# Two branch products in three fp32r passes, modulation chunks one merge sooner, the last norm by halves

## Chip, core and metric

The kernel runs on one core of one Trainium2 chip. The metric is the device time of one execution in microseconds (us), the lower the better. A core has a matrix engine (PE, with its weight loads listed apart as PEld), a vector engine (DVE), a scalar engine (ACT), a general engine (POOL) and SyncE (SP), whose queue issues nearly all DMAs here. The engines run their own instruction streams and meet only at semaphores. PE writes into eight PSUM banks of 128 x 512 fp32.

## What is computed

Two blocks of two layers each, on 256 tokens of width 1024, all in fp32. The change touches the first block and the last line of the second. One layer of the first block, cut to what matters:

```python
mod = c_act @ ada_w[l] + ada_b[l]                 # 3 x 1024 values: shift, scale, gate
h = rms_norm(x, pre_norm[l]) * (1 + scale) + shift
p = split_proj(h @ w_in[l])                       # projections, then "merge": 3 x 1024 columns
ret = rms_norm(retention(...)) * silu(p["ret_g"])     # [256, 512]
dsa = dsa_attention(...) * silu(p["dsa_g"])           # [256, 512]
gl  = rms_norm(gla(...)) * silu(p["gla_g"])           # [256, 512]
g = sigmoid(p["merge"]).reshape(B, S, 3, D)
y = g[:, :, 0] * (ret @ w_br_ret[l]) + g[:, :, 1] * (dsa @ w_br_dsa[l]) + g[:, :, 2] * (gl @ w_br_gla[l])
x = x + gate * rms_norm(y @ w_out[l], post_norm[l])
...
return rms_norm_2(x, final_g)                     # the last line of the second block
```

## The kernel before

**Weights.** All weights stream from HBM in chunks of up to 2 MB into a ring of three slots (`ring`). The table `RING1` names, for each layer of the first block, the 27 chunks in the order of loading, with width and slot. SP issues them in this order, one by one; ahead of each it waits until the chunk that held the slot has been used (`previous1`). A chunk whose slot is busy holds up all that stand behind it in SP's queue.

**Products.** An fp32 product of PE (`project`, and the branch products at L1081) reads a weight chunk as it is. A product in split passes reads three fp32r copies: ACT rounds the weights to a high part (L1605), DVE subtracts to get the rest (L2358), and PE adds high x high, rest x high and high x low in one bank (L1021). The merges from `SPLIT_FROM[l]` on (2 in layer 0, 1 in layer 1) are done so, in two halves of the k dimension; so are the output products. A merge chunk gives one 128 x 512 result for each of two token tiles (t = 0, 1), with banks chosen in `units_of_layer1`.

**Order.** The stage of interest is written out by hand. PE, ACT and DVE each run a loop over g = 0 to 17: g = 0 to 5 are the two tiles of ret_g, dsa_g and gla_g, g = 6 to 17 those of merge0 to merge5. In the gap after each g stand the small products of the three branches: the GLA scores `gla_scores(g)` go to banks 2 and 3, which DVE empties in `gla_take(g)` (L2300, L2305, L2309) before the next scores can start. At g = 11, 12, 13 PE transposes the results of retention, GLA and DSA (`retT`, `glaT`, `dsaT`), which ACT copies to SBUF. After the loop come the three branch products, br0, br1, br2.

**Modulation chunks.** The six chunks ada0 to ada5 of a layer compute `mod`: 0 to 3 shift and scale of the layer ahead, 4 and 5 the gate of this one. All six of layer 0, and 4 and 5 of layer 1, are summed by DVE (`chunk_sum`: L2067, then seven times L2070). Chunks 0 to 3 of layer 1 (`summed_on_pe`) go through PE ("rows", L719, 16 records), then a copy by ACT to SBUF. Either way PE then turns the sum into columns (`ada1`, L727, 8 records) and DVE adds them to `mod`. SP may reload the slot only when the sum is done. In the kernel before, chunk_sum(m) stands on DVE at merge m+1, and that of chunk 5 after the loop; the columns of chunk m follow merge m+1 on PE, and use bank 1, which merges 0 to 3 use too.

**Last norm.** For each token tile DVE adds two halves to X (L2498, L2500), ACT squares and sums the row of 1024 (L1885), DVE scales, ACT takes the root (L1887), DVE inverts and multiplies all 1024 columns (L2760), and SP stores 512 KB.

## Time and profile before

| | |
|---|---|
| median of 3 runs | 1077.6 us (1077.05 to 1078.86) |
| the profiled execution's own time | 1079.21 us |
| its span in the trace | 1077.4 us |
| mean granted clock of PE | 0.994 of full speed |
| PE busy (matmul) | 1042.0 us, 97% of the span |
| DVE, ACT busy | 601.1 us (56%), 477.9 us (44%) |
| branch products, layers 0 and 1 | 263.6 to 305.9 us, 566.6 to 608.9 us of the span |

The profiled execution was 1.6 us longer than the median of the timed runs. Its span leaves out 1.8 us around the program. PE's busy time is modelled from the starts of matmuls and overlaps, so pace is best read from start to start.

### The profile page before, as it was taken

Reading aid. Unit: us, or ns where it says so; the run is one execution under the profiler, and the core shown is the slowest. Engines: PE = TensorE matmul, PEld = TensorE weight load, DVE = VectorE, ACT = ScalarE, POOL = GpSimd, SP = SyncE. Lnnn points to the kernel's source line nnn. Section 1 sums busy time; section 2 is a strip of 40 time slices with the busy share of each in tenths; the row PEclk is TensorE's granted clock in tenths of the full one; section 3 lists DMA queues with packets and bytes.
Section 4 is the critical chain, followed back from the end, with each engine's and each line's share of the span. In section 5 each row is a group of like instructions: output and inputs, shape, how many; then the busy total and the mean of one; then the engine's idle time right before and its main releaser. Section 6 shows DMA issues by size and latency. Waiting matters only on the chain.

```text
span 1077.4 us, 13519 instructions
## 1 busy us (share of the span) xinstructions
PE 1042.0 (97%) x5208; PEld 757.8 (70%) x5208; DVE 601.1 (56%) x1177; ACT 477.9 (44%) x942; POOL 76.6 (7%) x103
## 2 busy tenths in 40 slices
PE   7999999999999999999999999999999999999997
PEld 5688875777467888857874587777677888556553
DVE  2429966595655299754454744236745555245742
ACT  3437547462134365476540353246535423225641
POOL 3001110000000020110000000500000001230000
PEclk9999999999999999999999999999999999999999
DMA  9645432476624355335467362422642015242000
GB/s 385 277 164 203 182 134 101 156 293 276 251 90 170 140 208 203 113 130 219 189 243 304 121 234 79 156 98 79 235 157 103 1 40 220 112 156 98 2 1 39
DMA packets 13743, 171.29 MB, mean 159 GB/s; under 512 B 1504, under 2 KB 1760, under 8 KB 3056
## 3 DMA queue, kind: packets, MB, share of 16 engines
q1 hardware_dynamic: 13216, 168.82, 41.0%
q10 hardware_dynamic: 464, 1.61, 0.4%
q8 instruction: 42, 0.69, 0.2%
q14 instruction: 21, 0.17, 0.0%
HBM read 169.37 MB, written 1.05 MB: 158 GB/s over the span
## 4 chain that ended last, share of the span: by engine, by line
PE 83%; DVE 7%; ACT 6%; DMA 2%; issue 1%; SPq 0%; DVEq 0%; ACTq 0%
PE bank L786 15%; PE bank L1132 8%; PE bank L1081 8%; PE bank L1021 7%; PE bank L1179 6%; PE bank L756 5%; PE bank L1138 5%; PE bank L1114 4%; PE bank L1316 3%; PE bank L764 3%; PE bank L866 3%; PE bank L1393 2%; PE bank L719 2%; PE bank L1381 1%; PE bank L727 1%
## 5 line engine op out<-in xcount | busy, mean ns | idle before, releaser
L1505 ACT ACTIVATE whi<-ring 128x512 fp32r<-128x512 f32 x120 | 73.6, 631 | 65.3 <-PE bank L786 65.3
L2169 DVE TENSOR_TENSOR wlo<-ring,whi 128x512 fp32r<-128x512 f32 x120 | 82.2, 708 | 32.8 <-ACT whi L1505 32.5
L786 PE MATMUL bank<-whi,xhi 128*128 128x512 f32 (+1 forms) x256 | 98.2, 384 | 1.3 <-ACT dsag L1428 1.3
L786 PE MATMUL bank<-wlo,xhi 128*128 128x512 f32 (+1 forms) x256 | 96.4, 377 | 0.0
L786 PE MATMUL bank<-whi,xlo 128*128 128x512 f32 (+1 forms) x256 | 96.4, 376 | 0.0
L764 PE MATMUL bank<-ring,hT 128*128 128x512 f32 (+1 forms) x160 | 61.2, 536 | 0.2 <-ACT hT L1448 0.2
L1138 PE MATMUL bank<-ring,hT 128*128 128x256 f32 (+2 forms) x224 | 57.9, 418 | 3.3 <-ACT hT L1471 2.3
L1021 PE MATMUL bank<-merge_high,xhi 128*128 128x512 f32 x144 | 58.2, 404 | 1.6 <-ACT retqkv L1428 1.1
L1021 PE MATMUL bank<-ring_low,xhi 128*128 128x512 f32 x144 | 56.9, 395 | 0.0
L1021 PE MATMUL bank<-merge_high,xlo 128*128 128x512 f32 x144 | 56.9, 395 | 0.0
L786 PEld LDWEIGHTS bank<-whi,xhi 128*128 128x128 f32 x256 | 48.2, 188 | 11.8 <-ACT dsag L1428 1.6
L786 PEld LDWEIGHTS bank<-whi,xlo 128*128 128x128 f32 x256 | 48.2, 188 | 8.9
L786 PEld LDWEIGHTS bank<-wlo,xhi 128*128 128x128 f32 x256 | 48.2, 188 | 8.2
L1138 PEld LDWEIGHTS bank<-ring,hT 128*128 128x128 f32 x224 | 38.9, 190 | 21.4 <-issue 16.3
L2358 DVE TENSOR_TENSOR ring_low<-ring,merge_high 128x1024 fp32r<-128x1024 f32 x36 | 42.5, 1222 | 18.7 <-ACT merge_high L1605 18.5
L1132 PE MATMUL bank<-ring_low,xhi 128*128 128x512 f32 x128 | 50.5, 394 | 0.0
L764 PEld LDWEIGHTS bank<-ring,hT 128*128 128x128 f32 x160 | 29.7, 190 | 26.4 <-issue 20.5
L1663 ACT ACTIVATE out_high<-ring 128x1024 fp32r<-128x1024 f32 x16 | 15.6, 1044 | 65.6 <-DMA ring<-in_weights 65.6
L2070 DVE SCALAR_TENSOR_TENSOR retqkv<-ring,cst,retqkv 128x512 f32<-128x512 f32 x56 | 42.1, 752 | 2.0
L1605 ACT ACTIVATE merge_high<-ring 128x1024 fp32r<-128x1024 f32 x36 | 36.0, 1052 | 9.6 <-PE bank L1021 9.6
L1132 PE MATMUL bank<-wide,xhi 128*128 128x512 f32 x96 | 39.0, 406 | 0.2 <-DVE ring_low L2520 0.2
L1179 PE MATMUL bank<-whi,xhi 128*128 128x512 f32 x96 | 38.5, 401 | 0.0
(414 smaller groups left out, 2198.3 us busy)
## 6 DMA issues: line engine op xcount, KB each, us to landing
ring<-in_weights SPq DMA_DIRECT2D x73, 2048.0 KB, 8.1
ring<-in_weights SPq DMA_DIRECT2D x5, 1024.0 KB, 5.0
ring<-in_weights SPq DMA_DIRECT2D x2, 1360.0 KB, 10.3
ring<-in_weights SPq DMA_DIRECT2D x1, 1536.0 KB, 8.3
kk<-in_k SPq DMA_DIRECT2D x1, 1120.0 KB, 7.7
X<-in_x SPq DMA_DIRECT2D x1, 1024.0 KB, 14.6
kc<-in_k ACTq DMA_DIRECT2D x1, 1024.0 KB, 10.6
X<-in_context SPq DMA_DIRECT2D x1, 1024.0 KB, 10.1
```

Of the source, the lines that this page charges most:

```text
L756: mm = pe.transpose(ps[0:n, i * P:(i + 1) * P], blk, ident[:])
L764: mm = pe.matmul(ps[:, 0:width], hT[:, k, t * P:(t + 1) * P], ring[:, slot, k * stride + w0:k * stride + w0 + width], start=(k == 0), stop ...
L786: mm = pe.matmul(o[:, 0:width], a, b[:, q % BUFFERS, at], start=(k == 0 and m == 0), stop=(k == KD - 1 and m == 2))
L1021: mm = pe.matmul(o[:, :], a, b, start=(k == 0 and n == 0), stop=(k == KD - 1 and n == 2))
L1081: mm = pe.matmul(ps[:, :], branchT[b][:, k, t * P:(t + 1) * P], ring[:, slot, k * D + h * 512:k * D + h * 512 + 512], start=(k == 0), stop ...
L1114: mm = pe.matmul(ps[:, :], a, b, start=(k == 0 and m == 0), stop=(k == KD - 1 and m == 2))
L1132: mm = pe.matmul(ps[:, :], a, b, start=(k == 0 and n == 0), stop=(k == KD - 1 and n == 2))
L1138: mm = pe.matmul(ps[:, 0:width], hT2[:, k, t * P:(t + 1) * P], ring[:, slot, k * width:(k + 1) * width], start=(k == 0), stop=(k == KD - 1))
L1179: mm = pe.matmul(o[:, :], a, b, start=(k == 0 and m == 0), stop=(k == KD - 1 and m == 2))
L1505: act.activation(whi1[:, q % BUFFERS, :], w, ACT.Copy).then_inc(event("hi1_ready"), 1)
L2169: dve.tensor_tensor(wlo1[:, q % BUFFERS, :], piece1(q)[2], whi1[:, q % BUFFERS, :], ALU.subtract).then_inc(event("lo1_ready"), 1)
L2358: dve.tensor_tensor(rest, w, whole, ALU.subtract).then_inc(event("merge_low"), 1)
```

## The change

It has four parts.

1. **br0 and br1 in split passes.** New tiles `ret_high`, `ret_low`, `dsa_high`, `dsa_low` hold the transposed results as fp32r parts: ACT writes the high part where it copied before, and DVE subtracts for the low part at g = 12 and g = 14 (`turned_rest`). The weights of br0 and br1 are rounded by ACT into `merge_high` (`branch_high`, in halves, the first at g = 17) and subtracted by DVE into `ring_low` (`branch_rest`). PE runs k outermost, with 3 passes for each of 2 tiles and 2 column halves. br2 stays fp32.
2. **Modulation chunks one merge sooner.** RING1 loads ada0 ahead of merge1 and so on, all ada chunks in slot 0, merges in slots 2 and 1 in turn. Rows, sums and columns move one merge up: chunk_sum(0) to g = 6, chunk_sum(m) to merge m, columns of chunk m after merge m, the last after br1. Columns of chunks 2 to 5 and the rows of chunk 3 get banks of their own.
3. **Order on DVE at the branches.** The multiplications of br0 stand behind the weight subtractions of br1, the output subtractions of half 0 ahead of those of br1's results, the last modulation columns behind them.
4. **Last norm by halves.** Squares, gain and stores by halves of 512 columns; the low half scaled by DVE, the high half by ACT.

The diff, cut:

```diff
-         ("dsa_g", KD * 512, 0), ("gla_g", KD * 512, 1), ("merge0", KD * 512, 2), ("merge1", KD * 512, 0),
-         ("ada0", KD * 512, 1), ("merge2", KD * 512, 2), ("ada1", KD * 512, 1), ("merge3", KD * 512, 0),
...
+         ("dsa_g", KD * 512, 0), ("gla_g", KD * 512, 1), ("merge0", KD * 512, 2), ("ada0", KD * 512, 0),
+         ("merge1", KD * 512, 1), ("ada1", KD * 512, 0), ("merge2", KD * 512, 2), ("ada2", KD * 512, 0),
+         ("merge3", KD * 512, 1), ("ada3", KD * 512, 0), ("merge4", KD * 512, 2), ("ada4", KD * 512, 0),
+         ("merge5", KD * 512, 1), ("ada5", KD * 512, 0), ("br0", 4 * D, 2), ("br1", 4 * D, 0), ("br2", 4 * D, 1),
...
+        if name == "gla_g1" and summed_on_pe(l, 0):
+            u.append(("s_ada0", 1))
...
+            if summed_on_pe(l, m + 1):
+                u.append((f"s_ada{m + 1}", (0, 0, 4)[m]))
+            if m < MERGES - 1:
+                u.append((f"ada{m}", (1, 1, 5, 2, 1)[m]))
+    for b, first in ((0, 4), (1, 0), (2, 5)):
+        u += [(f"br{b}{t}{h}", (first + 2 * t + h) % 8) for t in range(TT) for h in range(2)]
...
+                for b, name in enumerate(("retT", "dsaT")):
+                    for k in range(4):
+                        pe.wait_ge(event("branch_low"), 8 * l + 4 * b + k + 1)
...
+                                for n, (x1, x2) in enumerate(((hi, whole), (hi, rest), (low, whole))):
+                                    mm = pe.matmul(o[:, :], x1, x2, start=(k == 0 and n == 0), stop=(k == 3 and n == 2))
...
+                        if g == 17:
+                            branch_high(0, 0)
...
+                    if name == "gla_g" and summed_on_pe(l, 0):
+                        ada_out(u, "ada0", msum[0])
...
+                        if g in (12, 14):
+                            turned_rest((g - 12) // 2)
+                        if g == 17:
+                            branch_rest(0, 0)
                         if name[0:5] == "merge" and t == 0 and int(name[5]) > 0:
-                            chunk_sum(int(name[5]) - 1)
+                            chunk_sum(int(name[5]))
                         gla_sub(g + 2)
                         gla_mul(g + 1)
+                        if g == 6:
+                            chunk_sum(0)
...
+                act.activation(st2[:, 8 + t:9 + t], st2[:, 2 * t + 1:2 * t + 2], ACT.Sqrt, scale=1.0 / D,
+                               bias=st2[:, 4 + t:5 + t]).then_inc(event("f_std"), 1)
+                act.wait_ge(event("f_scale"), t + 1)
+                act.activation(Y2[:, t, 512:1024], Y2[:, t, 512:1024], ACT.Copy,
+                               scale=st2[:, 28 + t:29 + t]).then_inc(event("high_out"), 1)
```

How instructions move, at three places (line numbers are those of each kernel; in the kernel after, L2124 and L2127 are the chunk sum, L2366 the take, L2349 the GLA product, L1452 ACT's copy, L2390 and L2432 the subtractions for branches and merges, L2382 the new one for the transposed results).

DVE in layer 0 at g = 6 and 7, the kernel before:

```order
L2292 TENSOR_TENSOR Y<-gqT,Y 128x512 [waits gexp]
L2047 COPY cw<-ident 128x1 [waits bank_free2,bank_full2]
L2309 COPY_PREDICATED AT<-gm,bank 128x512
L2047 COPY cw<-ident 128x1 [waits bank_free3,bank_full3]
L2309 COPY_PREDICATED AT<-gm,bank 128x512
L2292 TENSOR_TENSOR Y<-gqT,Y 128x512 [waits gexp]
L2375 SCALAR_TENSOR_TENSOR L<-bank,sc 128x512 [waits bank_full4,sel_ready]
L2379 TENSOR_REDUCE mx<-L 128x2 [waits bank_free4]
L2375 SCALAR_TENSOR_TENSOR L<-bank,sc 128x512 [waits bank_full5]
L2379 TENSOR_REDUCE mx<-L 128x2 [waits bank_free5]
```

and after:

```order
L2349 TENSOR_TENSOR Y<-gqT,Y 128x512 [waits gexp]
L2124 TENSOR_SCALAR retqkv<-ring,cst 128x512 [waits slot_full0]
L2127 SCALAR_TENSOR_TENSOR retqkv<-ring,cst,retqkv 128x512 [waits dve_step] x7
L2104 COPY cw<-ident 128x1 [waits bank_free2,bank_full2]
L2366 COPY_PREDICATED AT<-gm,bank 128x512
L2104 COPY cw<-ident 128x1 [waits bank_free3,bank_full3]
L2366 COPY_PREDICATED AT<-gm,bank 128x512
L2349 TENSOR_TENSOR Y<-gqT,Y 128x512 [waits gexp]
L2455 SCALAR_TENSOR_TENSOR L<-bank,sc 128x512 [waits bank_full4,sel_ready]
L2459 TENSOR_REDUCE mx<-L 128x2 [waits bank_free4]
```

The sum of chunk 0 now stands between the GLA product for g = 7 and the take of the scores of g = 6, which frees banks 2 and 3.

ACT in layer 1 at g = 5 and 6, the kernel before (the rows from the three Silu calls on):

```order
L1641 ACTIVATE retg<-retg 128x1024 [waits bank_free1]
L1641 ACTIVATE dsag<-dsag 128x1024 [waits bank_free1]
L1641 ACTIVATE glag<-glag 128x1024 [waits bank_free1]
L1428 ACTIVATE G<-bank 128x512 [waits bank_full0,sel_ready]
L1559 ACT_TABLE_LOAD
L1559 ACTIVATE Y<-Y 128x512 [waits gsub]
L1428 ACTIVATE PT<-bank 128x512 [waits bank_full4]
```

and after:

```order
L1685 ACTIVATE retg<-retg 128x1024 [waits bank_free1]
L1685 ACTIVATE dsag<-dsag 128x1024 [waits bank_free1]
L1685 ACTIVATE glag<-glag 128x1024 [waits bank_free1]
L1452 ACTIVATE retqkv<-bank 128x512 [waits bank_full1]
L1452 ACTIVATE G<-bank 128x512 [waits bank_full0,sel_ready]
L1583 ACT_TABLE_LOAD
L1583 ACTIVATE Y<-Y 128x512 [waits gsub]
L1452 ACTIVATE PT<-bank 128x512 [waits bank_full4]
```

The copy that empties the rows of chunk 0 (into retqkv, from bank 1) stands behind the three Silu calls and ahead of merge0's copy.

DVE in layer 0 from g = 14 to the branch products, the kernel before:

```order
L2358 TENSOR_TENSOR ring_low<-ring,merge_high 128x1024 [waits merge_high] x2
L2067 TENSOR_SCALAR retqkv<-ring,cst 128x512 [waits slot_full1]
L2070 SCALAR_TENSOR_TENSOR retqkv<-ring,cst,retqkv 128x512 [waits dve_step] x7
L2358 TENSOR_TENSOR ring_low<-ring,merge_high 128x1024 [waits merge_high] x2
L2057 TENSOR_TENSOR mod<-bank,col 128x4 [waits bank_full1]
L2358 TENSOR_TENSOR ring_low<-ring,merge_high 128x1024 [waits merge_high] x2
L2067 TENSOR_SCALAR retqkv<-ring,cst 128x512 [waits slot_full1]
L2070 SCALAR_TENSOR_TENSOR retqkv<-ring,cst,retqkv 128x512 [waits dve_step] x7
L2067 TENSOR_SCALAR retqkv<-ring,cst 128x512 [waits slot_full1]
L2070 SCALAR_TENSOR_TENSOR retqkv<-ring,cst,retqkv 128x512 [waits dve_step] x7
L2057 TENSOR_TENSOR mod<-bank,col 128x4 [waits bank_full1]
L2424 TENSOR_TENSOR Y<-bank,G 128x512 [waits bank_free3,bank_full4,bank_free2,g_sig]
```

and after:

```order
L2432 TENSOR_TENSOR ring_low<-ring,merge_high 128x1024 [waits merge_high] x2
L2382 TENSOR_TENSOR dsa_low<-bank,dsa_high 128x4x128 [waits bank_full4,turned_high]
L2382 TENSOR_TENSOR dsa_low<-bank,dsa_high 128x4x128 [waits bank_full5,turned_high]
L2124 TENSOR_SCALAR retqkv<-ring,cst 128x512 [waits slot_full0]
L2127 SCALAR_TENSOR_TENSOR retqkv<-ring,cst,retqkv 128x512 [waits dve_step] x7
L2432 TENSOR_TENSOR ring_low<-ring,merge_high 128x1024 [waits merge_high] x2
L2114 TENSOR_TENSOR mod<-bank,col 128x4 [waits bank_full1]
L2432 TENSOR_TENSOR ring_low<-ring,merge_high 128x1024 [waits merge_high] x2
L2124 TENSOR_SCALAR retqkv<-ring,cst 128x512 [waits slot_full0]
L2127 SCALAR_TENSOR_TENSOR retqkv<-ring,cst,retqkv 128x512 [waits dve_step] x7
L2390 TENSOR_TENSOR ring_low<-ring,merge_high 128x1024 [waits branch_high] x4
L2390 TENSOR_TENSOR ring_low<-ring,merge_high 128x1024 [waits bank_free3,branch_high,bank_free2,g_sig]
```

Two new subtractions stand ahead of the sum at g = 14, and the sum of chunk 5 ahead of the first subtraction for br0's weights; before, DVE's next work behind that sum was the multiplications of br0's results.

## Rows read from the trace of the kernel before

**Rows 1.** The page's part 4: the chain that ended last, share of the span by engine.

```profile
PE 83%; DVE 7%; ACT 6%; DMA 2%; issue 1%; SPq 0%; DVEq 0%; ACTq 0%
```

**Rows 2.** Timeline of PE: start, length (us), engine, line, out<-in, shape, count.

```profile
251.72 0.49 PE L1021 MATMUL bank<-merge_high,xhi 128*128 128x512 f32 x1
...
278.19 13.98 PE L1081 MATMUL bank<-ring,glav 128*128 128x512 f32 x32
...
292.00 13.90 PE L1081 MATMUL bank<-ring,dsaqkv 128*128 128x512 f32 x32
```

**Rows 3.** Timeline of PE, rows with idle time before them [us <- releaser].

```profile
237.43 1.03 PE L727 MATMUL bank<-ones,retqkv 128*128 128x16 f32 x8 [1.36 <-ACT G L1428]
...
479.94 1.13 PE L979 MATMUL bank<-kdT,qdT 64*128 64x256 f32 x8 [0.63 <-ACT PT L1428]
...
488.04 0.50 PE L1021 MATMUL bank<-merge_high,xhi 128*128 128x512 f32 x1 [0.51 <-ACT retqkv L1428]
...
540.16 1.92 PE L719 MATMUL bank<-ring,cst 128*32 128x512 f32 x16 [1.01 <-ACT G L1428]
```

**Rows 4.** Timeline of DVE and PE in layer 0, g = 6 to 8.

```profile
178.61 0.69 DVE L2292 TENSOR_TENSOR Y<-gqT,Y 128x512 f32<-128x512 f32 x1
...
180.56 0.69 DVE L2292 TENSOR_TENSOR Y<-gqT,Y 128x512 f32<-128x512 f32 x1
...
186.52 5.48 DVE L2070 SCALAR_TENSOR_TENSOR retqkv<-ring,cst,retqkv 128x512 f32<-128x512 f32 x7
...
183.46 1.16 PE L949 MATMUL bank<-Y,KL 64*128 64x128 f32 x16
```

**Rows 5.** Timeline of PE and ACT in layer 1, g = 7 and the copy of merge0.

```profile
472.18 2.41 PE L764 MATMUL bank<-ring,hT 128*128 128x512 f32 x5
...
475.86 0.57 ACT L1428 ACTIVATE G<-bank 128x512 f32<-128x512 f32 x1
```

**Rows 6.** Timelines of DVE, SP, PE and ACT around merge4, merge5 and the branch products.

```profile
242.03 5.48 DVE L2070 SCALAR_TENSOR_TENSOR retqkv<-ring,cst,retqkv 128x512 f32<-128x512 f32 x7
...
247.53 3.90 SPq L665 DMA_DIRECT2D ring<-in_weights  x2
...
250.91 0.96 PE L727 MATMUL bank<-ones,retqkv 128*128 128x16 f32 x8
...
252.69 2.36 DVE L2358 TENSOR_TENSOR ring_low<-ring,merge_high 128x1024 fp32r<-128x1024 f32 x2 [0.62 <-ACT merge_high L1605]
...
255.42 0.49 DVE L2067 TENSOR_SCALAR retqkv<-ring,cst 128x512 f32<-128x512 f32 x1 [0.37 <-DMA ring<-in_weights]
...
262.75 0.96 PE L727 MATMUL bank<-ones,retqkv 128*128 128x16 f32 x8
...
275.53 0.33 SPq L665 DMA_DIRECT2D ring<-in_weights  x1
...
288.50 3.90 ACT L1663 ACTIVATE out_high<-ring 128x1024 fp32r<-128x1024 f32 x4 [24.95 <-DMA ring<-in_weights]
...
610.27 1.28 DVE L2450 TENSOR_TENSOR xlo<-bank,y_high 128x512 fp32r<-128x512 f32 x2
```

**Rows 7.** Busy time by stretch: us, PE, PEld, DVE, ACT, POOL, granted clock, DMA.

```profile
235.70:239.10 3.40, 2.04 (x16) 1.70 (x15) 2.29 (x3) 3.40 (x7) 0.00 (x0) 1.00 0.98 419
239.10:242.50 3.40, 3.40 (x10) 2.64 (x9) 3.23 (x4) 1.05 (x2) 0.00 (x0) 0.52 1.03 443
...
646.00:649.50 3.50, 2.49 (x16) 2.02 (x14) 0.90 (x3) 1.35 (x4) 0.00 (x0) 1.00 0.02 10
```

**Rows 8.** Timelines of ACT, DVE and SP at the last norm; the first row is from layer 1.

```profile
617.96 0.60 ACT L1677 ACTIVATE L<-bank 128x512 f32<-128x512 f32 x1 [4.85 <-PE bank L1114]
...
1071.26 1.06 ACT L1885 ACTIVATE Y<-X 128x1024 f32<-128x1024 f32 x1 [11.07 <-DVE X L2500]
...
1073.06 1.28 DVE L2760 SCALAR_TENSOR_TENSOR Y<-X,st,gbr 128x1024 f32<-128x1024 f32 x1
...
1074.37 0.34 SPq L694 DMA_DIRECT2D out<-Y  x1
```

More of the change, by code:

```diff
@@ L692, in _ @@
             for t in range(TT):
[L693 to L695 removed]
+                for h in range(2):
+                    c = slice(h * 512, (h + 1) * 512)
+                    sp.wait_ge(event(("low_out", "high_out")[h]), t + 1)
+                    sp.dma_start(out[0, t * P:(t + 1) * P, c], Y2[:, t, c]).then_inc(stored, 16)
+            sp.wait_ge(stored, 32 * TT)
         def arrived0(eng, m):
@@ new lines, in _ @@
+                ada1(l, MERGES - 1)
+                slot = landed("br2")
+                for t in range(TT):
+                    emptied(pe, u, f"glaT{t}")
+                    for h in range(2):
+                        ps = begin(u, f"br2{t}{h}")
+                        for k in range(4):
+                            mm = pe.matmul(ps[:, :], glaT[:, k, t * P:(t + 1) * P],
+                                           ring[:, slot, k * D + h * 512:k * D + h * 512 + 512],
+                                           start=(k == 0), stop=(k == 3))
+                        done(u, f"br2{t}{h}", mm)
@@ L2316, in _, with turned_rest, branch_rest @@
                 gla_sub(1)
+                def turned_rest(b):
+                    for t in range(TT):
+                        dve.wait_ge(event("turned_high"), (2 * l + b) * TT + t + 1)
+                        name = ("retT", "dsaT")[b]
+                        ps = filled(dve, u, f"{name}{t}")
+                        c = slice(t * P, (t + 1) * P)
+                        dve.tensor_tensor(turned_low[b][:, :, c], ps[:, :].rearrange("p (k c) -> p k c", k=4),
+                                          turned_high[b][:, :, c], ALU.subtract).then_inc(free(u, f"{name}{t}"), 1)
+                def branch_rest(b, half):
+                    for i in (2 * half, 2 * half + 1):
+                        w, whole, rest = branch_piece(b, i)
+                        dve.wait_ge(event("branch_high"), 8 * l + 4 * b + i + 1)
+                        dve.tensor_tensor(rest, w, whole, ALU.subtract).then_inc(event("branch_low"), 1)
                 def chunk_sum(m):
```

149 lines of the change are left out of this document (84 added, 65 removed).

## The prediction

> **What bounds the kernel now.** I read the chain of waits first: PE carries 83% of it, DVE and ACT 13% together, DMA 2% [rows 1]. So the time moves with two things: how long PE's own work takes, and where PE stands still. Then I read PE's timeline for the pace of each form of product and for its waits. In the first block's merge and branch stages PE waits only a few times and briefly [rows 3], always for ACT or DVE to empty a bank or deliver a weight. Last I read DVE, ACT and SP around those places, because three parts of the change add work or move it there, and the stretches of PE's clock, since it fell once in this stage.
>
> **Part 1, the passes.** An fp32 product shows as two records. br1 has 16 products (32 records) and runs from 278.19 to 292.00: 13.8 us, 0.86 us each [rows 2]. A product in split passes costs three records, and a merge has exactly as many as a branch will have: 2 tiles x 8 k x 3 = 48, from 251.72 to 262.75, 11.03 us [rows 2, 6]. A branch has 4 k x 2 tiles x 2 halves x 3 = 48 of the same shape. So each branch gains 2.8 us, and four of them (two in each layer) 11.1 us. All of it is on PE and so on the path. Neither operand changes its shape, so I see no reason for another pace.
>
> What feeds it: ACT's roundings and DVE's subtractions of 128x1024, 1.2 us each [rows 6]. While br0 runs, DVE stands free in the kernel before, so for br1, and for the second half of br0, they are hidden: each k of a branch gives PE 2.8 us. The first half of br0 is not, see part 2. The rest of the transposed results costs DVE 1.3 us (two 128x512 from PSUM, like L2450) at g = 12 and again at g = 14 [rows 6].
>
> Behind br0 the order is harmless. The multiplications of br0 wait for four subtractions, but their banks (4 to 7) are wanted next only after br1. The last columns follow br1 and cost the same there.
>
> **Part 2, chunks one merge sooner.** The work is the same; what counts is whom it holds up.
>
> *Layer 0, g = 6.* The sum of chunk 0 goes ahead of the take of the scores of g = 6. DVE reaches that point at 179.2 (L2292 ends), the take is over at 180.56, and PE wants the two banks at 183.46 for the scores of g = 7 [rows 4]. So there are 2.9 us of slack. The sum takes 0.5 + 5.5 = 6.0 us [rows 4, 6]. PE waits 6.0 - 2.9 = 3.1 us. Nothing covers it: behind the scores stands merge1.
>
> *Layer 1, g = 7.* The rows of chunk 0 now use bank 1 after gla_g, and merge0's second tile wants it next. ACT empties it only behind its Silu calls, where before it copied merge0, at 475.86, and 0.57 us long. PE would be there at 472.18 plus the moved rows, 1.9 us like those at 540.16, = 474.1 [rows 3, 5]. So PE waits 2.3 to 2.4 us; I take 2.4. The wait of 0.63 us behind it (L979) is absorbed, and the 0.51 at 488.04 goes, as another bank is used [rows 3].
>
> *End of merge5.* This is the main one. SP may load ada5 only when the sum of chunk 4 is done, and DVE now sums chunk 5 ahead of the first subtraction of br0's weights. From the end of one sum to the end of the next: 7.9 us landing (issue 247.53, use 255.42), 6.0 us sum, then 1.2 us subtraction, 15.1 us until PE can start br0 [rows 6]. PE itself needs, from the end of merge4 (250.91), the columns and merge5, 11.8 us (262.75). If sum and merge4 end together, PE waits 3.3 us. Before, that sum (then of chunk 3) ended at 247.5, 3.4 us ahead of merge4's end; 1.7 of these came from the slow clock (below), and the new subtraction takes 1.3. So 0.4 is left, and in layer 0 PE waits 2.9 us. In layer 1 there was no sum at g = 14; now two subtractions (2.4), two new ones (1.3) and a sum (6.0) stand there, 9.7 us, which start some 2 us into merge4's 11.0. I put the end 1.0 us behind merge4 (bounds 0 and 1.3, the size of the new subtractions): PE waits 1.0 for the columns and 3.2 for br0. The other input, br0's transfer, lands at nearly the same time: two transfers issued within 2 us took 13.0 us to the second's landing (275.53 to 288.50) [rows 6], plus rounding and subtraction 2.2, again 15.2. So removing one wait alone would not help.
>
> *What goes.* The 1.36 us at 237.43 and the 1.01 at 540.16 are waits for bank 1 which new banks end [rows 3]. In layer 0, though, DVE has had no pause since g = 10, and the new 1.3 us delays dsa's last multiplication, so PE's transposes wait about 1.3 instead: nothing won.
>
> Sum of waits: layer 0 +3.1 +2.9 +1.3 -1.4 = +5.9; layer 1 +2.4 +1.0 +3.2 -0.6 -0.5 -1.0 = +4.5. Together +10.4 us.
>
> **Part 3, the last norm.** From DVE's last addition (1071.2) to the issue of the store at 1074.37 pass 3.1 us: a square of 1.06 and more, three small steps, a product of 1.28 [rows 8]. By halves the square is 0.6, DVE's scaling of a variance leaves the path, and the last product is 0.6. The second store then goes out at about 1073.4. I take -1.0 us (bounds -0.5, if each store pays its whole latency, and -1.3). A pointer as scale on ACT: the copy of 128x512 took 0.60 here without one [rows 8]. The Trainium skill (ScalarE: Activation LUTs, What ACT_TABLE_LOAD costs) gives each per-partition operand about 93 ns more; by it the gain would be 0.9.
>
> **The clock.** In the stretch 235.7 to 239.1 PE was busy for only 2.04 us of 3.4, with one wait of 1.36 us and narrow transposes and columns; in the next 3.4 us the granted clock was 0.52, that is 1.2 in place of 2.4 GHz, and PE did half of its work: 1.7 us lost. At 646.0, busy 2.49 of 3.5, it stayed at 1.00 [rows 7]. The new waits of 3.1, 2.9 and 3.2 us are about twice the one that a fall followed, so I give each a fall with a chance of about 0.75, and the 2.4 one half; these chances are a choice, as two stretches are little to go by. Expected: 2 to 3 falls where there was one. I take three, +3.4 us.
>
> (The Trainium skill, TensorE: Matmul & The Clock Gate, HAM oscillation, tells of a kernel whose waits for transfers slowed the clock again and again. [...])
>
> **The sum.** -11.1 -1.0 +10.4 = -1.7 with the clock as before; with two more falls +1.7. The profiled execution is 1079.21 us and gives 1080.9; it lies 1.6 above the median, about one fall of the clock, so the timed runs may hold none. I apply the change to the median: 1077.6 + 1.7 = **1079.3 us**. With two falls in place of three it is 1077.6.
>
> **Rivals.**
> 1. *The gain comes through in part.* If the waits cost half (DVE gets to the sums sooner, ada5 lands sooner), the change is -1.7 -5.2 and with one fall more +1.7: 1072.4; with the waits a quarter smaller and no more falls, 1073.3. For it: each wait is a difference of long chains. Against: all terms are rows, and the orders leave no choice. Chance 0.22.
> 2. *Slower: the clock.* PE falls to 1.2 GHz after all five waits: five falls for one, +6.8 -1.7 = +5.1: 1082.7; with four, 1081.0. It decides from four falls on. For it: the fall behind 1.36 us [rows 3, 7]. Against: no fall at 646.0, with PE idle for 1.0 us of 3.5. Chance 0.30.
> 3. *Waits hidden.* Only the passes and the norm count: 1077.6 - 12.1 = 1065.5. Against it speaks DVE's row at 186.52, the length of a sum. Chance 0.06.
> 4. *The passes give nothing,* because three weight loads per product slow PE: 1077.6 + 11.1 + 1.7 = 1090.4. The merges at the same shape speak against it. Chance 0.02.
>
> **How the numbers follow.** My forecast, two or three falls, has 0.40. The bound of what a measurement of this kernel can tell from no change is 0.2%, 2.2 us: 1075.4 to 1079.8. Forecast: nearly all inside. Rival 1 and 3 faster, 0.28, with 0.01 from the forecast's edge; rivals 2 and 4 slower, 0.32. The range reaches from rival 1's middle to rival 2's top: 1071.5 to 1082.7, leaving out rivals 3, 4 and the ends.
>
> **What the profile after would show.** br0 and br1 at 11 us each, against 13.8; DVE's first chunk sum in layer 0 straight before L2366, with PE idle some 3 us before its scores; PE idle 2.4 us before merge0's second tile in layer 1, released by ACT; PE idle about 3 us before br0 in both layers, released by DVE's subtraction; stretches at half clock behind these; the last issue of a store 2.2 us behind the last addition. I am wrong if br0 follows merge5 without a pause, or if the scores of g = 7 do.

## Result and profile after

| | before | after |
|---|---|---|
| median of the timed executions | 1078.4 us (18 runs, 1076.91 to 1082.95) | 1083.2 us (18 runs, 1081.14 to 1090.79) |
| ratio | | 1.0047, 95% interval 1.0036 to 1.0059 |
| the profiled execution, and its span | 1079.21, 1077.4 us | 1084.83, 1083.0 us |
| mean granted clock of PE in it | 0.994 | 0.985 |

The change made the kernel slower by 0.47%, about 5 us. The forecast was 1079.3 in a range up to 1082.7: the time lies 0.5 us above the range, whose top was the second rival's (the clock) worst case. (The last norm is part 4 in the list of the change; the prediction and one expectation call it part 3.)

The chain of waits of the kernel after, shares of the span by engine; it answers to [rows 1]:

```profile
PE 78%; DVE 9%; ACT 7%; DMA 4%; issue 2%; SPq 0%; DVEq 0%; ACTq 0%
```

PE has lost 5 points: DVE and DMA have 2 more each, ACT and issue 1 each. Where it stands still, PE's waits between 100 and 660 us say (engine, line waited for: us in total, times, longest us):

```profile
PE bank L956 <- DVE AT L2366: 4.1, 1, 4.1
PE bank L1095 <- DVE ring_low L2390: 3.6, 2, 2.3
PE bank L771 <- ACT retqkv L1452: 2.4, 1, 2.4
...
PE bank L763 <- DVE dsag L2419: 0.8, 1, 0.8
PE bank L734 <- DVE retqkv L2127: 0.8, 1, 0.8
```

The lines left out are waits that the kernel before has too. These five are the waits of the prediction, one by one: the scores of g = 7, br0 (twice), merge0's second tile in layer 1, dsa's transposes, the columns of chunk 4 in layer 1. PE's timeline at these places (start us, us, engine line op out<-in xcount [idle before <-releaser]):

```profile
185.75 2.08 PE L956 MATMUL bank<-Y,KL 64*128 64x128 f32 x16 [4.06 <-DVE AT L2366]
...
189.49 9.42 PE L771 MATMUL bank<-ring,hT 128*128 128x512 f32 x16
...
200.36 7.13 PE L771 MATMUL bank<-ring,hT 128*128 128x512 f32 x16
...
272.04 0.50 PE L1095 MATMUL bank<-merge_high,ret_high 128*128 128x512 f32 x1 [2.33 <-DVE ring_low L2390]
...
481.47 10.21 PE L771 MATMUL bank<-ring,hT 128*128 128x512 f32 x16 [2.39 <-ACT retqkv L1452]
...
563.71 1.06 PE L734 MATMUL bank<-ones,retqkv 128*128 128x16 f32 x8 [0.79 <-DVE retqkv L2127]
...
578.90 0.50 PE L1095 MATMUL bank<-merge_high,ret_high 128*128 128x512 f32 x1 [1.23 <-DVE ring_low L2390]
```

The rows at 189.49, 200.36 and 481.47 are eight products (16 records) each, all of one form. They take 7.13 us at full clock, and 9.42 and 10.21 us behind two of the waits. The windows between 100 and 660 us in which PE ran at half clock (us, busy time and count of PE, PEld, DVE, ACT, POOL, then the granted clock, DMA share, GB/s):

```profile
183.90:194.15 10.25, 8.39 (x30) 5.62 (x31) 8.02 (x18) 2.19 (x8) 0.00 (x0) 0.50 0.88 346
245.35:248.76 3.41, 3.41 (x9) 2.62 (x9) 3.20 (x5) 2.00 (x3) 0.00 (x0) 0.50 1.02 437
272.65:276.07 3.42, 3.42 (x10) 2.64 (x9) 2.83 (x3) 1.89 (x2) 0.00 (x0) 0.50 0.91 374
480.87:487.70 6.83, 6.23 (x8) 2.62 (x9) 6.05 (x14) 5.80 (x9) 1.28 (x1) 0.50 0.00 0
566.20:569.61 3.41, 3.41 (x10) 2.63 (x9) 2.07 (x2) 0.00 (x0) 0.00 (x0) 0.50 0.97 413
```

Here is what I had not foreseen. Three of the five falls stand where I expected them, but the first lasts 10.2 us and the fourth 6.8, not 3.4 each. The other two, at 245.35 and 566.20, stand behind waits of 0.80 and 0.79 us, to which I had given none. Together it is 27.3 us at half clock, where the kernel before had 3.4 in this stage [rows 7]. (Both traces also have 3.4 us at half clock near the start, ahead of 35 us, and some more at the very end.)

The trace adds up. From layer 0's product that waits 0.64 us for ACT's dsag (at 149.30 before, 147.47 after) to layer 1's that waits 1.58 us for ACT's hT (650.07 and 657.36) the time grew by 9.1 us. The rows of the passes and the waits give -2.2 (the table near the end, without the norm). PE was busy for 24.9 us of the half clock, 21.5 more than before, which costs half of that, 10.7. That makes +8.5 of the 9.1.

**All timed executions.** Each lists its span and its mean clock, and span x (1 - clock) is what it lost in time of full clock. That splits a time in two: the clock, and all the rest.

| mean of the timed executions | lost to the clock | the rest |
|---|---|---|
| before (82 runs beside the experiments) | 5.0 us | 1074.0 us |
| after (18 runs) | 13.1 us | 1070.8 us |
| difference | +8.1 | -3.2 |

So but for the clock the change does gain. How much depends on the split: within one kernel's executions a microsecond of lost clock lengthens the time by only some 0.75 us, since some of it is lost where it costs nothing, as at the very end. At that rate the 8.1 us cost about 6, and the gain without them is about 1 us, not 3.2. (The rest scatters by 0.9 to 1.7 us between executions, as a standard deviation. The profiled execution lost 16 us to the clock, more than the mean of 13.1.)

### The profile page after: what moved, and what is told of

Read it like the earlier page. It is cut to its first block, busy times and chain, and to the rows that moved or that the text cites. A ratio compares the mean times of both kernels' runs of the same rounds, so it can differ in the third digit from the quotient of the medians.

```text
span 1083.0 us, 13715 instructions
## 1 busy us (share of the span) xinstructions
PE 1042.3 (96%) x5272; PEld 774.4 (72%) x5272; DVE 625.0 (58%) x1205; ACT 495.7 (46%) x964; POOL 76.5 (7%) x103
## 3 DMA queue, kind: packets, MB, share of 16 engines
HBM read 169.37 MB, written 1.05 MB: 157 GB/s over the span
## 4 chain that ended last, share of the span: by engine, by line
PE 78%; DVE 9%; ACT 7%; DMA 4%; issue 2%; SPq 0%; DVEq 0%; ACTq 0%
PE bank L793 14%; PE bank L1156 8%; PE bank L1203 6%; PE bank L763 5%; PE bank L1162 5%; PE bank L1095 4%; PE bank L1138 4%; PE bank L771 4%; PE bank L1028 3%; DVE retqkv L2127 3%; PE bank L1340 3%; PE bank L1107 3%; PE bank L873 3%; DMA ring<-in_weights 2%; PE bank L1417 2%; PE bank L726 2%
## 5 line engine op out<-in xcount | busy, mean ns | idle before, releaser
L771 PE MATMUL bank<-ring,hT 128*128 128x512 f32 (+1 forms) x160 | 66.6, 572 | 2.6 <-ACT retqkv L1452 2.4
L793 PEld LDWEIGHTS bank<-whi,xhi 128*128 128x128 f32 x256 | 48.2, 188 | 11.9 <-ACT dsag L1452 1.6
L2432 DVE TENSOR_TENSOR ring_low<-ring,merge_high 128x1024 fp32r<-128x1024 f32 x36 | 42.5, 1222 | 12.9 <-ACT merge_high L1629 12.8
L2127 DVE SCALAR_TENSOR_TENSOR retqkv<-ring,cst,retqkv 128x512 f32<-128x512 f32 x56 | 43.0, 768 | 2.0
L2597 DVE TENSOR_TENSOR ring_low<-ring,whi 128x1024 fp32r<-128x1024 f32 x12 | 15.6, 1303 | 39.1 <-ACT whi L1766 39.1
```

What stands on the lines that cost most here:

```text
L771: mm = pe.matmul(ps[:, 0:width], hT[:, k, t * P:(t + 1) * P], ring[:, slot, k * stride + w0:k * stride + w0 + width], start=(k == 0), stop ...
L793: mm = pe.matmul(o[:, 0:width], a, b[:, q % BUFFERS, at], start=(k == 0 and m == 0), stop=(k == KD - 1 and m == 2))
L2127: ins = dve.scalar_tensor_tensor(rows, w, cst[:, k, v:v + 1], rows, ALU.mult, ALU.add)
```

## Experiments

Ratios are to the kernel before in the same series, whose median was 1078.2 to 1079.2; differences between kernels below are taken from the ratios. The last two columns split the mean as above; each mean is uncertain by 0.4 to 1.3 us for the clock and by 0.3 to 0.6 for the rest (standard errors).

| kernel | median us | ratio (95% interval) | clock | rest |
|---|---|---|---|---|
| after | 1083.2 | 1.0047 (1.0036 to 1.0059) | 13.1 | 1070.8 |
| take first | 1080.7 | 1.0026 (1.0009 to 1.0042) | 11.9 | 1069.4 |
| copy first | 1080.2 | 1.0021 (1.0007 to 1.0035) | 10.9 | 1070.1 |
| both | 1078.0 | 0.9991 (0.9979 to 1.0002) | 9.2 | 1068.1 |
| both, later subtraction | 1075.5 | 0.9968 (0.9953 to 0.9983) | 8.9 | 1066.7 |
| the same with fillers | 1074.0 | 0.9951 (0.9933 to 0.9969) | 6.0 | 1068.0 |
| the same with more fillers | 1072.7 | 0.9948 (0.9929 to 0.9966) | 4.1 | 1068.9 |
| after, long fillers | 1081.9 | 1.0032 (1.0020 to 1.0045) | 5.6 | 1077.0 |
| after, short fillers | 1080.4 | 1.0016 (1.0003 to 1.0029) | 7.8 | 1072.8 |
| before, passes alone | 1079.1 | 1.0007 (0.9995 to 1.0019) | 7.5 | 1072.2 |
| before, norm alone | 1077.6 | 0.9984 (0.9969 to 0.9999) | 4.5 | 1073.3 |
| before, chunks alone | 1086.4 | 1.0080 (1.0055 to 1.0105) | 9.1 | 1078.2 |
| before, one filler | 1079.1 | 1.0001 (0.9984 to 1.0017) | 5.5 | 1074.1 |

### Is it the long waits that slow the clock?

First I took away two of the waits, each by one move.

```diff
-                        if g == 6:
-                            chunk_sum(0)
...
                         if g < len(LEVELS):
                             gla_take(g)
+                        if g == 6:
+                            chunk_sum(0)
```

> The changed kernel with one move: in layer 0 DVE takes the scores of g = 6 first and sums chunk 0 behind them. Theory (the waits are as large as summed, but each long one is followed by several stretches at 1.2 GHz): PE's wait of 4.06 us before the scores of g = 7 goes, and with it the 10.2 us at half clock behind it, which cost 5.1 us: 9.2 us less than the changed kernel, 1074.0. Rival A (the fall of the clock belongs to this stage and comes whether PE waits or not): only the wait goes, -4.1, 1079.1. Rival B (the sum only moves its delay to the next step of DVE, the logits of g = 7): a new wait of 2 to 4 us at the transposes of g = 8 and a time within 2 us of 1083.2.

Measured: 1080.7, by the ratios 2.3 us less than after, where the theory had 9.2, and less than rival A's 4.1 too. It is nearest to rival B, with the new wait in another place. The trace says why:

```profile
185.05 1.06 PE L734 MATMUL bank<-ones,retqkv 128*128 128x16 f32 x8 [1.97 <-DVE retqkv L2127]
...
267.69 0.50 PE L1095 MATMUL bank<-merge_high,ret_high 128*128 128x512 f32 x1 [3.62 <-DVE ring_low L2390]
```

The scores no longer wait, but the columns of chunk 0 stand right behind them, and now they wait 1.97 us for the same sum. I had looked at the next step of DVE and not at the next one of PE. The clock still falls once behind it, for 3.4 us in place of 10.2 (in this trace; over all executions the clock lost 11.9 us in place of 13.1, a difference within the scatter, so the 10.2 us of one trace overstate what there was to win on the mean). And the wait before br0 has grown from 2.33 to 3.62 us: PE gets there sooner, but DVE and the transfers do not.

```diff
                             head_roots("r", 8)
+                            if summed_on_pe(l, 0):
+                                ada_out(u, "ada0", msum[0])
                             for dst in (retg, dsag, glag):
...
-                    if name == "gla_g" and summed_on_pe(l, 0):
-                        ada_out(u, "ada0", msum[0])
```

> The changed kernel with one move: in layer 1 ACT copies the rows of chunk 0 ahead of its three Silu calls. Theory: the wait of 2.39 us before the second tile of merge0 goes, and the 6.8 us at half clock behind it (3.4 us lost): 5.8 us less, 1077.4. The Silu calls start 0.6 us later, which costs nothing. Rival A (the fall comes anyway): -2.4, 1080.8. Rival B (the copy ahead of the table load delays DVE's norm of retention and with it another wait of PE): less than 1 us gained.

Measured: 1080.2, 2.8 less, of 5.8; the measurement can't tell it from rival A's 2.4. The wait of 2.39 us is gone from the trace and so is the slow stretch behind it. The wait before br0 in layer 1, 1.23 us in after, is now 3.01, with 6.8 us at half clock around it.

> The changed kernel with both moves, DVE's take of the scores ahead of the sum in layer 0 and ACT's copy ahead of the Silu calls in layer 1. Theory: the two gains add, -9.2 -5.8 = -15.0: 1068.2, which is 10 us faster than the kernel before. Left are the waits before br0 (2.3 and 1.2) with one fall each. Rival A: -4.1 -2.4: 1076.7. If a wait is only pushed on, the sum of the two gains is missed by as much as it measures in the trace.

Measured: 1078.0. The two gains do add (2.3 + 2.8, and 6.0 us in one kernel), but to less than half of the 15.0 expected and close to rival A's 6.5, the waits alone. With both the kernel is as fast as the one before. Mean clock lost is 9.2, still 4 us more than there.

### The clock by itself

Taking a wait away changes two things. To change mainly the clock, I left the waits on the other engines and gave PE small products of ones to do inside them.

```diff
+                    if l == 0 and g == 7:
+                        emptied(pe, u, "ro1")
+                        keep_busy(bank[7], 33)
                     if g < len(LEVELS):
                         gla_scores(g)
...
+                keep_busy(begin(u, "br000"), (19, 10)[l])
                 for b, name in enumerate(("retT", "dsaT")):
```

> The changed kernel with small products of ones on PE inside three of its waits, each a little shorter than the wait: 33 before the scores of g = 7 in layer 0 (wait 4.06 us), 19 and 10 before br0 in layers 0 and 1 (2.33 and 1.2 us). All waits on other engines stay as they are. Theory: PE's position is the same, but the clock stays at 2.4 GHz behind them: of 10.2 + 3.4 + 3.4 us at half clock 8.5 us are won back, 1074.7; the stretch of 6.8 us in layer 1 stays. Rival A (the clock does not depend on PE being idle): no change, 1083.2, or up to 0.5 slower. Rival C (the clock falls once at each place all the same, only the repeats go): -3.4 to -5, 1078 to 1080.

The fillers were too long. A product of ones is two records and takes 0.23 us, not the 0.12 that I had read for one record:

```profile
187.23 7.59 PE L757 MATMUL bank<-ones 128*128 128x128 f32 x66
```

That is 7.6 us in a wait of 4.06. The time says little, then (1081.9, with a rest of 1077.0), but the clock says what was asked. From 100 to 660 us, the first block, the granted clock is 1.00 throughout:

```profile
100.00:660.00 560.00, 547.96 (x2860) 423.88 (x2859) 382.68 (x718) 282.21 (x521) 26.45 (x25) 1.00 0.48 183
```

and the mean loss over all executions falls from 13.1 to 5.6 us, near the 5.0 of the kernel before. Rivals A and C, a clock that does not heed the idle time or falls once all the same, are out. The waits of 2.39 and 0.8 us, which have no fillers in this version, were followed by no fall in this trace either. I then took 16, 9 and 5 products.

> The run with products of ones in the waits again, with the right number of them: one product took 0.23 us there, so that 33 and 19 lasted 7.6 and 4.4 us against waits of 4.06 and 2.33, and PE came 3.5 and 2.1 us late (it measured 1081.9). Now 16 before the scores of g = 7 (3.7 us), 9 and 5 before br0 (2.1 and 1.2 us). Theory: PE's place is that of the changed kernel, and the falls of the clock behind these three waits stay away, as they did in the longer version: 10.2 + 3.4 + 3.4 us at half clock, 8.5 us: 1074.7. From the longer version the same sum gives 1081.9 - 5.6 = 1076.3. Rival (the clock needs more activity than the filler gives, or falls elsewhere instead): 1081 to 1083.

Measured: 1080.4, 3.3 us less than after where the theory had 8.5, and just below the rival's 1081 to 1083: 7.8 us lost to the clock, 5.3 less, and 2.0 more in the rest. In the trace the three filled waits have no fall behind them; two falls of 3.4 us are left, behind waits of 2.40 and 0.79 us that were not filled. In layer 1 the wait before br0 was 1.23 us; here it is 1.16 us of fillers and another 1.80 behind them:

```profile
573.35 0.50 PE L1099 MATMUL bank<-merge_high,ret_high 128*128 128x512 f32 x1 [1.80 <-DVE ring_low L2394]
```

So a slow stretch ahead of a wait is partly paid by that wait. PE comes late, and then waits less. That is one reason why each repair above brought only a quarter to a half of its sum. The other is that the sums took the falls of one execution, one with more lost clock than the mean, for those of all.

### What each part is worth

> The kernel before with part 3 alone, the last norm by halves. Theory: -1.0 us (bounds -0.5 and -1.3), 1077.2; the trace shows some 2.2 us from DVE's last addition to the issue of the last store, in place of 3.1. Rival (two stores for one, each with its own latency): no gain or +0.5.

Measured: ratio 0.9984, which is -1.7 us by the medians (interval -0.1 to -3.3) and holds the theory's -1.0; 0.7 us less in the rest. In the kernel after, ACT's last square, DVE's last product and the issue of the last two stores:

```profile
1077.98 0.63 ACT L1936 ACTIVATE Y<-X 128x512 f32<-128x512 f32 x1 [6.14 <-DVE X L2582]
```
```profile
1079.39 0.49 DVE L2846 TENSOR_SCALAR Y<-Y,st 128x512 f32<-128x512 f32 x1
```
```profile
1079.90 0.81 SPq L701 DMA_DIRECT2D out<-Y  x2
```

From the start of the square to the end of the span are now 1083.0 - 1077.98 = 5.0 us. It was 1077.4 - 1071.26 = 6.1 [rows 8], so 1.1 less. The last store of after is issued at 1080.28, 2.3 us behind the start of the square; before it was 3.1.

For the passes alone, the kernel before got part 1 and the new order at the branches, with the sum of chunk 5 between the pairs of subtractions:

```diff
                         if m == MERGES - 1:
+                            branch_rest(0, 1)
                             chunk_sum(m)
...
+                branch_rest(1, 0)
+                branch_rest(1, 1)
                 for b in range(3):
```

> The kernel before with part 1 alone: br0 and br1 in split passes, with DVE's order at the branches; chunks, their sums and columns stay where they stood, the last norm too. Chunk 5 is summed between the two pairs of subtractions. It prices the passes by themselves, and with them what part 2 took. Theory: the four branches give 2.8 us each, -11.1; none of the waits at g = 7, before merge0's second tile or at the columns is there, but the first weights of br0 still land late, since they wait for merge4's slot: 1 to 3 us before br0 in each layer, with a fall of the clock behind each (+1.7): 1078.2 - 11.1 + 4 + 3.4 = 1074.5. So the passes alone beat the kernel before by 2 to 6 us, and part 2 took about 9. Rival (part 2 is what lets the passes start in time, without it PE waits 6 us and more before br0): 1079 or more.

Measured: 1.0007, no change, where the theory had 4 us less. The time is the rival's (1079 or more), but not its cause, a wait of 6 us and more before br0. The theory erred in the place. br0 does start nearly on time, but PE now waits ahead of br1, and inside it (layer 0, then layer 1):

```profile
278.77 0.50 PE L1094 MATMUL bank<-merge_high,dsa_high 128*128 128x512 f32 x1 [2.69 <-DVE ring_low L2380]
...
282.78 0.80 PE L1094 MATMUL bank<-merge_high,dsa_high 128*128 128x512 f32 x1 [0.72 <-DVE Y L2495]
...
581.74 0.50 PE L1094 MATMUL bank<-merge_high,dsa_high 128*128 128x512 f32 x1 [1.07 <-DVE ring_low L2380]
...
585.75 0.50 PE L1094 MATMUL bank<-merge_high,dsa_high 128*128 128x512 f32 x1 [1.65 <-DVE Y L2495]
```

DVE's queue of layer 0 shows what stands there:

```profile
266.20 2.36 DVE L2380 TENSOR_TENSOR ring_low<-ring,merge_high 128x1024 fp32r<-128x1024 f32 x2 [0.50 <-ACT merge_high L1650]
271.43 0.49 DVE L2114 TENSOR_SCALAR retqkv<-ring,cst 128x512 f32<-128x512 f32 x1 [2.87 <-DMA ring<-in_weights]
271.95 5.48 DVE L2117 SCALAR_TENSOR_TENSOR retqkv<-ring,cst,retqkv 128x512 f32<-128x512 f32 x7
```

The sum of chunk 5 waits 2.87 us for its transfer and takes 6.0, and the weights of br1 stand behind it. The other wait (L2495) is for br0's multiplications, since the bank table of before gives br1's last result the bank of br0's first. So the passes alone gain 1.8 us in the rest, of 11, and lose 2.5 to the clock. That points to a use of part 2, which takes chunk 5 away from br1; no run tried another place for chunk 5 in this order.

> The kernel before with part 2 alone: chunks, rows, sums and columns one merge sooner, and the order of the last columns and of the output subtractions that goes with it; br0 and br1 stay fp32, the last norm too. Theory: the waits at g = 7, at merge0's second tile and at the columns stay as in the changed kernel (4.1 + 2.4 + 0.8 us), two waits of the kernel before go (1.4, 1.0), br0 starts when it has landed: +5 us, and behind the two long waits the clock falls for 10 to 17 us, another 4 to 6 us on the mean: 1087 to 1089. Rival (the parts add up: passes alone gave 0, the norm -0.8, all together +4.8, so part 2 alone is +5.6): 1084. A result near 1084 would mean that half of the time at half clock is made up for elsewhere.

Measured: 1086.4, a ratio of 1.0080: just under the theory's 1087 to 1089 and above the rival's 1084. The interval, 1084.1 to 1089.5, holds the theory's range and all but reaches the rival. The theory's waits are there, but for the one at the columns, and the waits before br0 are now for its transfer:

```profile
186.29 2.08 PE L946 MATMUL bank<-Y,KL 64*128 64x128 f32 x16 [4.06 <-DVE AT L2310]
...
267.85 2.41 PE L1080 MATMUL bank<-ring,retqkv 128*128 128x512 f32 x5 [1.11 <-DMA ring<-in_weights]
...
480.85 7.13 PE L761 MATMUL bank<-ring,hT 128*128 128x512 f32 x16 [2.40 <-ACT retqkv L1427]
```

The rest is 4.2 us above the kernel before (expected 5), the clock 4.1. Alone the parts cost 8.6 (chunks), 0.8 (passes) and -1.7 us (norm), 7.7 together, and in one kernel 5.1; with the intervals of these runs the difference is not shown. Look at the last row: the same wait of 2.40 us as in after at 481.47, but the products behind it take 7.13 us, not 10.21. A wait of this length does not always bring the clock down. The wait of 4.06 us at 186.29 was followed by 6.8 us at half clock here, and by 10.2 in after.

```diff
+                        if l == 0 and m == 3:
+                            keep_busy(begin(u, "merge40"), 5)
                         if m > 0:
                             ada1(l, m - 1)
```

> The kernel before with one addition: in layer 0 PE has 5 products of ones (1.2 us) in its wait of 1.36 us ahead of the columns of chunk 2, at 237.4. Theory: the 3.4 us at half clock that follow this wait in the trace stay away, -1.7 us in an execution that has them; as the timed executions lose 4.7 to 5.2 us of clock on the mean and 3.4 of it lies at the start and the end, the median moves by -0.5 to -1.7. Rival (the fall comes from the narrow products around it, not from the wait): no change.

Measured: no change, 1.0001, and 5.5 us lost to the clock. The time is the rival's, but the trace speaks against its cause: the slow stretch behind 237.4, which the traces of before and of the norm alone both have, is gone. Another stands behind the next wait, one that the kernel before did not have:

```profile
265.15 1.07 PE L727 MATMUL bank<-ones,retqkv 128*128 128x16 f32 x8 [1.07 <-DVE retqkv L2072]
```
```profile
239.10:242.50 3.40, 3.18 (x22) 2.80 (x22) 2.16 (x4) 3.40 (x6) 0.00 (x0) 1.00 1.01 429
267.05:270.46 3.41, 3.41 (x6) 1.34 (x5) 0.00 (x0) 0.00 (x0) 0.00 (x0) 0.51 0.96 399
```

With its clock up PE came to DVE's sum too early, waited 1.07 us and was slowed there. In this trace one filler only moved the fall.

### A version that beats both

```diff
-                        if g in (12, 14):
-                            turned_rest((g - 12) // 2)
+                        if g in (12, 16):
+                            turned_rest((g - 12) // 4)
```

> Both moves, and the subtraction for the transposed dsa result at g = 16 in place of g = 14, no fillers. Beside the version with both moves alone (ratio 0.9991) it prices the later subtraction, beside the one with fillers (0.9951) it prices the fillers. Theory: ada5 is loaded 1.3 us sooner, but br0 lands hardly sooner (the two transfers share the DMA engines): -0.5 to -1.3, and the falls of the clock stay: 1076.5 to 1077.5, ratio 0.998 to 0.999, with 9 us of lost clock. Rival (the later subtraction was what helped, the fillers nothing): 0.995.

Measured: 1075.5, ratio 0.9968, 2.5 us less than both moves alone by the ratios of the medians, and 1.7 less by the means. I had 0.5 to 1.3. PE's gates of layer 1 and the start of br0, with both moves:

```profile
448.93 0.47 PE L793 MATMUL bank<-whi,xhi 128*128 128x512 f32 x1 [0.65 <-ACT dsag L1452]
...
569.20 0.50 PE L1095 MATMUL bank<-merge_high,ret_high 128*128 128x512 f32 x1 [1.28 <-DVE ring_low L2390]
```

and with the later subtraction:

```profile
448.12 0.47 PE L793 MATMUL bank<-whi,xhi 128*128 128x512 f32 x1 [0.65 <-ACT dsag L1452]
...
567.34 0.80 PE L1095 MATMUL bank<-merge_high,ret_high 128*128 128x512 f32 x1 [2.98 <-DVE ring_low L2390]
```

From one to the other are 120.3 and 119.2 us: br0 starts 1.05 us sooner (in layer 0 it is 0.9). The wait is longer all the same, because PE gets there sooner: the slow stretch of 3.4 us ahead of it (1.7 us) and the wait of 0.79 us at the columns, both in the trace with both moves, are gone from this one. So the transfers do start sooner by nearly the whole 1.28 us of the subtraction.

> Both moves (DVE's take ahead of the sum in layer 0, ACT's copy ahead of the Silu calls in layer 1), and two additions: the subtraction for the transposed dsa result stands at g = 16, ahead of the sum of chunk 5, in place of g = 14 ahead of the sum of chunk 4; and PE has 8 products of ones (1.8 us) in the wait of 1.97 us that was left before the columns of chunk 0, and 8 before br0 in layer 0 (wait 3.4 us). Theory: with both moves alone it was 1078.0 (profiled 1073.4 of span, three falls of 3.4 us in this stage). The later subtraction starts ada5's load 1.3 us sooner, which shortens both waits before br0, -1.3 -1.0; two or three falls stay away, -3.4 to -5.1: 1071 to 1073. Rival (the wait before br0 is the landing of both transfers, not the sum): -0 in place of -2.3, 1073 to 1075.

Measured: 1074.0, clock 6.0 in place of 8.9. That is above the theory's 1071 to 1073. The 1.8 us between it and the same version without fillers (1075.5) is within the intervals, so these fillers are shown to hold the clock, not to save time. The rival had the time, but its cause (a later subtraction that gives nothing) is out by the run above. The two limits on br0 show in one place here, ACT waiting for br0's transfer and DVE for the sum of chunk 5, 1.1 us apart:

```profile
566.01 2.00 ACT L1655 ACTIVATE merge_high<-ring 128x1024 fp32r<-128x1024 f32 x2 [9.96 <-DMA ring<-in_weights]
```
```profile
567.10 2.36 DVE L2394 TENSOR_TENSOR ring_low<-ring,merge_high 128x1024 fp32r<-128x1024 f32 x2
```

> The version with both moves, the later subtraction and fillers (1074.0, ratio 0.9951), with 10 products of ones before br0 in layer 0 in place of 8 and 12 in layer 1 in place of none. There its trace had a wait of 2.96 us and 6.8 us at half clock behind it. Theory: the wait stays, since br0 lands only then, but the clock stays up: -3.4 in an execution like the profiled one, less on the mean of many, since a fall does not come in each: 1072 to 1073, and a share of lost clock near 5 us. Rival (fillers delay PE as much as they save): 1074 to 1075.

Measured: 1072.7, ratio 0.9948 with an interval of 0.9929 to 0.9966: 5.6 us faster than the kernel before, and 10.7 than the kernel after. The edit is 10 and 12 in `keep_busy(begin(u, "br000"), ...)` and 8 ahead of the columns of chunk 0. It can't be told from the 1074.0 of the version with fewer fillers. PE's rows in front of br0 in layer 1, and the first block as a whole:

```profile
562.91 2.84 PE L757 MATMUL bank<-ones 128*128 128x128 f32 x24
566.02 0.50 PE L1099 MATMUL bank<-merge_high,ret_high 128*128 128x512 f32 x1 [0.27 <-DVE ring_low L2394]
```
```profile
100.00:660.00 560.00, 551.11 (x2842) 425.45 (x2841) 384.30 (x713) 283.74 (x526) 26.57 (x25) 1.00 0.49 187
```

No half clock is left in it. Against the version without fillers they took 4.8 us of lost clock (8.9 to 4.1) and gave 2.2 back in the rest, as found above; the time is 2.2 us lower by the ratios, with overlapping intervals, so what the fillers gain on top of the moves is not shown.

## Why the prediction was wrong

The sum, term by term, against the trace after:

| term | predicted | measured |
|---|---|---|
| four branches in passes | -11.1 | -10.3 |
| last norm | -1.0 | -1.1 in the trace, -0.7 on the mean |
| waits of layer 0 | +3.1 +2.9 +1.3 -1.4 | +4.06 +2.33 +0.80 -1.36 |
| waits of layer 1 | +2.4 +1.0 +3.2 -2.1 | +2.39 +0.79 +1.23 -2.15 |
| all of it, clock left out | -1.7 | -3.3; by the executions -3.2 |
| clock | +3.4 | +8.1 by the executions, +10.7 in the trace |
| sum | +1.7 | +4.9 |

**Passes: right.** In layer 1, at full clock, br0 starts at 578.90 (above); the start of br1 and of what follows:

```profile
590.20 0.40 PE L1095 MATMUL bank<-merge_high,dsa_high 128*128 128x512 f32 x1
...
601.40 0.96 PE L734 MATMUL bank<-ones,retqkv 128*128 128x16 f32 x8
```

11.3 and 11.2 us against 13.8 [rows 2]: 2.5 or 2.6 each, where I took 2.8.

The measured change is, by the ratio, the second rival's +5.1. The range was missed by 0.5 us because it also stood on a base 0.8 us too low: the median of 3 runs, 1077.6, where 18 gave 1078.4. That is chance. The forecast's +1.7 is not saved by it.

**Waits: right in place and cause, all six.** The scores of g = 7 wait 1.0 us longer than worked out, since the sum in front of the take ran longer (see the last section). The 2.39 was foreseen at 2.4. The waits before br0 came out smaller in the trace of after, 2.33 and 1.23 for 2.9 and 3.2, because slow stretches ahead of them held PE up; with the clock up they measured 3.46 and 3.01 (copy first) and 3.62 (take first). In the sum I had taken clock and waits as independent. They are not, and this made the two waits too large by 2.5 us together. Two small waits were 0.7 us less than summed; against that stand the passes (0.8 less gained) and the scores (1.0 more), so the sum without the clock came out 1.6 us too high; at 0.75 us per us of lost clock the executions would put it at about -1, near the -1.7.

**The clock: the step that failed.** I gave each long wait at most one fall of 3.4 us, and took three falls in all, +3.4 us, since the trace of before showed one such fall behind one wait [rows 3, 7]. The number of places came out at the upper end, five: behind three of the long waits (g = 7, merge0's second tile, br0 of layer 0), and behind two of 0.8 us, at dsa's transposes and at the columns of layer 1, to which I had given none. Two of the five lasted three and two times as long, and the term is 8.1 us on the mean of the executions in place of 3.4. That PE's idle time does it, and not the work beside it, rests on the fillers: with three waits filled, and nothing else changed, 13.1 us of loss became 7.8, and 5.6 with longer ones.

The fourteen traces together give a better price than my two stretches did. Between 100 and 660 us they have 20 waits of PE of 1.9 us or more, and 17 of these had half clock behind them (it began inside the wait or up to 2 us after it), for 3.4 to 10.2 us. Of 63 waits of 0.7 to 1.9 us, 10 had it, within 2.5 us. No fall stands without such a wait ahead of it. Why the same wait of 2.4 us had 6.8 us at half clock behind it in one trace, 3.4 in two and nothing in two others stays open; no run here tells.

(The Trainium skill, TensorE: Matmul & The Clock Gate, HAM oscillation, describes such repeated falls for a kernel whose waits for transfers lasted 3 to 5 us. The trace agrees where a wait here was as long, though for DVE: half clock came with the 4.06 us, inside the wait or just behind it, in all three traces without fillers that have it. The falls behind waits of 0.8 to 2.4 us are not in that account; they rest on the rows of this case alone.)

**The rivals.** The first (waits half as large) is out: they were there. The third and fourth are out too. The second had 0.30 and should have had more than the forecast. It speaks of five waits, though its sum has only four of more than 2 us, and it too gave each wait one fall of 3.4 us: five falls, +6.8, where the measured term is +8.1. That it names five falls, and the trace has five, is luck in part, since two of them stand behind waits of 0.8 us.

## What to carry to other kernels

A new wait of the matrix engine of 2 us or more costs itself and, in most traces here, clock behind it: three such waits and three of 0.8 to 1.2 us cost 8.1 us of lost clock on the mean of executions, worth about 6 us of time. Before letting a change pass that adds such waits, ask whether the work in front of the releasing step can stand behind it (two such moves gave 6 us here), and then what the engine waits for next. Where a wait can't go, small products of no use in it can hold the clock: keep them shorter than the wait, and look at the next wait too, since one filler alone moved the fall there. In the kernel after they saved 3.3 us; on top of the moves a gain in time was not shown. And split times into clock and rest over all executions before explaining one trace.

## What the runs showed of the hardware

**A slow stretch can be two or three times as long as another.** In the stage each lasted 3.4, 6.8 or 10.2 us. In the longest PE was busy for 8.4 us, and it went on for 4.7 us after 189.49, where PE had nothing but full products. The head of the program, which no version changes, shows the same spread: half clock began at 27 to 28.5 us and lasted 3.4 us in the trace of before, and 10.2 us in those of the long fillers, of both moves with fillers, and of the kernel before with one filler.

**DVE runs slower beside POOL.** The sum that frees the scores' banks, with the step ahead of it, and POOL's only operation of that stretch:

```profile
177.38 0.48 DVE L2124 TENSOR_SCALAR retqkv<-ring,cst 128x512 f32<-128x512 f32 x1
177.89 6.36 DVE L2127 SCALAR_TENSOR_TENSOR retqkv<-ring,cst,retqkv 128x512 f32<-128x512 f32 x7
```
```profile
177.60 1.38 POOL L2027 TENSOR_TENSOR KL<-gkT,Y 128x512 f32<-128x512 f32 x1 [14.20 <-ACT Y L1583]
```

All other sums of this kernel in layer 0 take 5.47 or 5.48 us. Four other traces with this order (copy first, both versions with fillers alone, chunks alone) have 6.36 or 6.37 at this place too. In the run with the take first, the sum starts behind POOL's operation and takes 5.48 too:

```profile
179.51 5.48 DVE L2127 SCALAR_TENSOR_TENSOR retqkv<-ring,cst,retqkv 128x512 f32<-128x512 f32 x7
```

So I put 0.9 us of the 4.06 down to POOL; no run moved POOL alone. (The Trainium skill, SBUF — State Buffer, SBUF: two separate sides, has the two engines share a port pair as an exclusive lock, also for a DVE operation with two inputs in SBUF against a POOL operation that reads SBUF, as here. The trace agrees in size, roughly: POOL runs for 1.09 us of the sum, which is 0.88 longer.)

**A pointer as scale on ACT** makes the copy of 128x512 0.72 us, where the one without took 0.60 [rows 8]:

```profile
1079.39 0.72 ACT L1943 ACTIVATE Y<-Y,st 128x512 f32<-128x512 f32 x1 [0.30 <-DVE st L2844]
```
